# First attention on paired PSUM banks, the convolution's projection four outputs at a time, and the first gathered rows later

## The chip, the cores and the metric

The kernel runs on one core of a Trainium2 chip. Its engines work beside one another, each through its own list of instructions: TensorE (PE) multiplies matrices, VectorE (DVE), ScalarE (ACT) and GpSimd (POOL) do the rest, and the queue of SyncE (SP) issues most transfers. Semaphores alone order them. The metric is the device time of one execution, in microseconds; lower is better.

## The reference

Two transformer blocks on 512 tokens of width 1024, in fp32. The parts that the change touches are in the first:

```
q, k, v, u, ga, gc = split(h @ w_in)               # q: 8 heads, k and v: 2 heads, 256 more keys from the context
p = softmax(q k^T * 128 ** -0.5)                   # 768 keys
y_att = (p v) @ w_attn_o
g = a * sigmoid(b);  g = depthwise_conv(g, 31 taps) + conv_b        # a, b = split(u)
y_conv = silu(layernorm(g)) @ w_conv_o
x = x + g1 * ((sigmoid(ga) * y_att + sigmoid(gc) * y_conv) @ w_out)
x = x + g2 * peer_ffn(modulate(rmsnorm(x)))        # 16384 experts, 128 chosen for each token
```

shift, scale and g1, g2 come from silu(c) @ w_mod, 48 rows of 128. Then a second block of attention (block-sparse and differential) follows, which the change leaves as it is.

## The kernel before

Nearly all products are made as three: each fp32 operand is split into a high half (rounded to fp32r) and a low half (the rest), and TensorE adds high·high, high·low and low·high (mm3, L708). So every weight chunk of 128x1024 goes through a ring: SP loads it into one of 4 raw buffers (L551), ACT makes the high half Rh (ahead, L1236), POOL or DVE makes the low half Rl (lows, L1735; low_half, L1826), and TensorE uses it in 24 matmuls (gemm_T, L720). Rh and Rl have 5 slots. LOW_DVE names the chunks whose low half DVE makes. Rows of w_mod pass through the same raw buffers and are reduced on DVE (modulation, L1875). The order of all chunks is the list of stream_plan; the bank, the count of fills and the count of reads of each PSUM use are worked out ahead in psum_plan.

**First attention.** 32 steps, one for a head and 128 queries. In step n TensorE turns the weights P of step n (turn1), makes the scores of step n+2 (scores1, 512 and 256 columns in two banks), does one whole projection of 24 matmuls if the step has a job (attention_jobs: 12 chunks of w_u for the convolution, 11 of w_g for the gates), and every second step multiplies by the values (values1). DVE finds the maximum of each score row in scores1, hands the negative to ACT (semaphore neg), later the reciprocal of the sum (finish1, pinv). ACT takes the exponential (exps1), divides (normed1), copies the turned weights out (turned1), and empties the job's bank: gate for w_g, glu_gate for the sigmoid half of w_u. Between its steps DVE works through the taps of the depthwise convolution, 31 for each of 8 channel blocks, by tap(), 217 of them in these 32 steps. All jobs use bank 6, so a job starts only when the last one's bank has been emptied.

**Behind it.** w_ao (8 chunks) projects the attention. DVE does the last 31 taps, TensorE sums over channels with a matrix of ones for the mean (mu), DVE subtracts, ACT squares, TensorE sums again (var), DVE and ACT make rsd, and then per channel block DVE multiplies by rsd (cn), ACT does silu and the high half XAh (cRh), DVE and POOL in turn the low half XAl. w_co needs all 8 blocks of XA for each of its 8 outputs. merge_att multiplies the outputs of w_ao by the gates sga. Gates are kept in DRAM meanwhile (store_gate) and come back as sga and sgc, 2 MB each.

**Expert layer.** 128 experts' rows for each of the first 128 tokens are gathered by GpSimd, 4 KB a partition, 0.5 MB a gather, into 7 buffers (gather, L1778): 128 of u, then 128 of v. DVE takes them one by one (gathered, L2380 and L2388). The other 384 tokens go through dense products with all 128+128 chunks, in 16 groups (m) of 12 chunks (n); product and product_low (L2348, L2353) make the moving operand XG, whose high half ACT makes (weighed, L1555). GATHERED says how many rows DVE has taken behind each chunk.

## Time and profile before

| | |
|---|---|
| median of 3 runs | 2286.78 us (2285.72 to 2289.66) |
| the profiled execution | 2285.51 us, span 2283.7 us |
| PE busy | 2139.4 us, 94% |
| PE weight loads busy | 1832.0 us, 80% |
| DVE busy | 1698.7 us, 74% |
| ACT busy | 942.9 us, 41% |
| POOL busy | 964.6 us, 42% |
| granted TensorE clock, mean | 0.978 |
| DMA, mean | 200 GB/s |

"Busy" counts an engine's own instructions; the line numbers are those of the kernel before. A matmul's length in the profile overlaps the next one's, so TensorE's pace is read from the distance between starts. The granted clock is the share of full speed at which TensorE ran.

### The profile page before, as it was taken

Reading aid. Unit: us, or ns where it says so; the run is one execution under the profiler, and the core shown is the slowest. Engines: PE = TensorE matmul, PEld = TensorE weight load, DVE = VectorE, ACT = ScalarE, POOL = GpSimd, SP = SyncE. Lnnn points to the kernel's source line nnn. Section 1 sums busy time; section 2 is a strip of 40 time slices with the busy share of each in tenths; the row PEclk is TensorE's granted clock in tenths of the full one; section 3 lists DMA queues with packets and bytes.
Section 4 is the critical chain, followed back from the end, with each engine's and each line's share of the span. In section 5 each row is a group of like instructions: output and inputs, shape, how many; then the busy total and the mean of one; then the engine's idle time right before and its main releaser. Section 6 shows DMA issues by size and latency. Waiting matters only on the chain. (4 is left out here: it accounts for less than half of the span.)

```text
span 2283.7 us, 29764 instructions
## 1 busy us (share of the span) xinstructions
PE 2139.4 (94%) x10685; PEld 1832.0 (80%) x10685; DVE 1698.7 (74%) x3444; ACT 942.9 (41%) x1544; POOL 964.6 (42%) x633
## 2 busy tenths in 40 slices
PE   6998899896989999989989999999999999899988
PEld 3886677665768999989978988888988888777767
DVE  5876887887460999999868888887888887745243
ACT  3445555434233443444423333333333333445572
POOL 0341122124434565789944444444444542442222
PEclk9999999998999999999999999999999999899999
DMA  7332011154632454546799999999999996221111
GB/s 297 102 93 74 33 61 65 44 187 155 232 131 91 143 162 153 173 153 225 264 359 360 350 336 333 352 353 339 360 359 340 350 359 221 97 80 57 39 56 47
DMA packets 177137, 455.84 MB, mean 200 GB/s; under 512 B 13792, under 2 KB 80736, under 8 KB 175328
## 3 DMA queue, kind: packets, MB, share of 16 engines
q1 hardware_dynamic: 136912, 293.57, 37.7%
q0 software_dynamic: 36864, 134.23, 15.8%
q10 hardware_dynamic: 3216, 26.15, 3.0%
q8 instruction: 86, 1.41, 0.2%
...
## 5 line engine op out<-in xcount | busy, mean ns | idle before, releaser
L1735 POOL TENSOR_TENSOR Rl<-raw,Rh 128x1024 fp32r<-128x1024 f32 x171 | 447.8, 2624 | 795.4 <-ACT Rh L1236 795.0
L709 PE MATMUL bank<-XAh,Rh 128*128 128x384 f32 (+1 forms) x1472 | 537.2, 365 | 38.1 <-POOL Rl L1735 15.3
L1236 ACT ACTIVATE Rh<-raw 128x1024 fp32r<-128x1024 f32 x380 | 399.9, 1056 | 338.5 <-DMA raw<-in_u 108.9
L711 PE MATMUL bank<-XAh,Rl 128*128 128x384 f32 (+1 forms) x1472 | 523.0, 355 | 0.0
L710 PE MATMUL bank<-XAl,Rh 128*128 128x384 f32 (+1 forms) x1472 | 522.8, 355 | 0.0
L709 PEld LDWEIGHTS bank<-XAh,Rh 128*128 128x128 f32 x1472 | 281.3, 191 | 61.6 <-issue 20.0
L710 PEld LDWEIGHTS bank<-XAl,Rh 128*128 128x128 f32 x1472 | 281.3, 191 | 18.2
L711 PEld LDWEIGHTS bank<-XAh,Rl 128*128 128x128 f32 x1472 | 280.3, 190 | 18.4
L1778 POOL DMA_INDIRECT ga<-in_v,eid x128 | 181.3, 1416 | 204.4 <-DVE y L2388 187.0
L1778 POOL DMA_INDIRECT ga<-in_un,eid x128 | 172.7, 1349 | 220.9 <-DVE act L2380 197.1
L1826 DVE TENSOR_TENSOR Rl<-raw,Rh 128x1024 fp32r<-128x1024 f32 x197 | 242.1, 1229 | 2.5 <-ACT Rh L1236 2.5
L1055 PE MATMUL bank<-Rh,XGh 128*128 128x512 f32 x744 | 230.2, 391 | 2.6 <-issue 2.6
L1057 PE MATMUL bank<-Rl,XGh 128*128 128x512 f32 x744 | 229.8, 390 | 0.0
L1059 PE MATMUL bank<-Rh,XGl 128*128 128x512 f32 x744 | 229.7, 390 | 0.0
L2047 DVE SCALAR_TENSOR_TENSOR cout<-gb,vecs,cout 128x512 f32<-128x512 f32 x240 | 206.2, 859 | 2.1
L709 PE MATMUL bank<-Rh,XAh 128*128 128x512 f32 x416 | 166.3, 400 | 3.4 <-DVE Rl L1826 1.8
L2388 DVE SCALAR_TENSOR_TENSOR y<-ga,act,y 128x1024 f32<-128x1024 f32 x127 | 163.1, 1284 | 2.5
L1055 PEld LDWEIGHTS bank<-Rh,XGh 128*128 128x128 f32 x744 | 139.9, 188 | 30.9 <-issue 2.9
L2380 DVE CUSTOM_DVE_ANT_0 ga<-ga,x 128x1024 f32<-128x1024 f32 x128 | 154.3, 1218 | 13.4 <-DMA ga<-in_un,eid 13.4
L1057 PEld LDWEIGHTS bank<-Rl,XGh 128*128 128x128 f32 x744 | 140.0, 188 | 29.4
L1059 PEld LDWEIGHTS bank<-Rh,XGl 128*128 128x128 f32 x744 | 140.0, 188 | 29.3
L711 PE MATMUL bank<-Rh,XAl 128*128 128x512 f32 x416 | 162.8, 391 | 0.0
...
## 6 DMA issues: line engine op xcount, KB each, us to landing
raw<-in_u SPq DMA_DIRECT2D x128, 512.0 KB, 8.3
raw<-in_v SPq DMA_DIRECT2D x128, 512.0 KB, 6.2
...
```

The lines of the kernel that those rows point to most:

```text
L709: e.matmul(o, sh, mh, start=first, stop=False)
L710: e.matmul(o, sh, ml, start=False, stop=False)
L711: return e.matmul(o, sl, mh, start=False, stop=last)
L1055: e.matmul(o[i][:, :], XGh[:, x, tok], hi[:, 512 * i:512 * i + 512], start=first, stop=False)
L1057: e.matmul(o[i][:, :], XGh[:, x, tok], lo[:, 512 * i:512 * i + 512], start=False, stop=False)
L1059: t = e.matmul(o[i][:, :], XGl[:, x, tok], hi[:, 512 * i:512 * i + 512], start=False, stop=False)
L1236: e.activation(Rh[:, r % NRING, :], raw[:, n % NRAW, :], ACT.Copy).then_inc(s["hi"], 1)
L1735: e.tensor_tensor(Rl[:, r % NRING, :], raw[:, n % NRAW, :], Rh[:, r % NRING, :].bitcast(F32), ALU.subtract).then_inc(s["lo"], 1)
L1778: e.indirect_dma_start(ga[n % NGB][:, :], None, table[:, :], bass.IndirectOffsetOnAxis(ap=eid[:, n % 128:n % 128 + 1], axis=0)).then_inc(s ...
L1826: e.tensor_tensor(Rl[:, r % NRING, :], raw[:, c % NRAW, :], Rh[:, r % NRING, :].bitcast(F32), ALU.subtract).then_inc(s["lov"], 1)
L2047: ins = e.scalar_tensor_tensor(out=o, in0=g[:, j:j + 512], scalar=vec("taps", 31 * cb + j), in1=o, op0=ALU.mult, op1=ALU.add)
L2388: t = e.scalar_tensor_tensor(out=y0[:, :], in0=v, scalar=act0[:, j:j + 1], in1=y0[:, :], op0=ALU.mult, op1=ALU.add)
```

## The change

Six edits:

1. The scores of a step lie in one tensor of two banks (pair). DVE takes the negated maximum of all 768 columns in one instruction, ACT one exponential with one sum; the factor 128^-0.5 is multiplied into the gain of q beforehand. The addition of two sums and the maximum of two maxima go.
2. In a step with a job ACT empties the job's bank first and makes the next high half after that. The job of step 0 comes ahead of the first turn on TensorE; the job w_g 15 moves from step 27 to step 31 and has a buffer of its own (pkg3).
3. The low halves of w_ao 3 to 7, w_co 0 to 7 and w_o 0 and 1 move from POOL to DVE, and stand between its taps and layer-norm steps. POOL no longer makes low halves of XA.
4. w_mod rows are read at other places, w_ao 2 and 3 are loaded ahead of sga. TensorE does seven of the w_ao products ahead of mu and none between mu and var.
5. w_co 0 to 3 are worked on together, block by block of XA (24 matmuls become 12 for each of 8 blocks, over four banks), the others one after another.
6. GpSimd gathers rows 5 and later only when the first product is done, and DVE takes one row ahead of it instead of four; the three rows are caught up in groups 4, 6 and 11, in which DVE takes one row more each.

```diff
-    for m, n in zip(range(5, 16), (0, 2, 3, 8, 12, 13, 17, 18, 22, 26, 27)):
+    for m, n in zip(range(5, 16), (0, 2, 3, 8, 12, 13, 17, 18, 22, 26, 31)):
...
-    for i, w in enumerate(("w_ao", "w_co", "w_o", "w_pq")):
-        for m in range(8):
-            p += [(w, m), ("w_mod", 16 + 8 * i + m)]
+    for m in range(8):
+        p += [("w_ao", m), ("w_mod", 16 + m)]
+    p += [("w_co", m) for m in range(4)]
+    for m, mods in zip(range(4, 8), ((24, 25), (26, 27), (28, 29), ())):
+        p += [("w_mod", n) for n in mods] + [("w_co", m)]
+    for m in range(8):
+        p += [("w_o", m)] + [("w_mod", n) for n in ((30 + 2 * m, 31 + 2 * m) if m < 2 else (32 + m,))]
+    for m in range(8):
+        p += [("w_pq", m), ("w_mod", 40 + m)]
...
+        if _m == 0 and _n < 4:
+            _k = (0, 0, 0, 1)[_n]
+        if _m in (4, 6, 9, 10, 11, 12, 13) and _n == 2:
...
+    def scores(n):
+        use(("s", n, 0), 2 * (n % 2), 1, 2)
+        use(("s", n, 1), 2 * (n % 2) + 1, 0, 0)
...
-LOW_DVE = set(range(8)) | set(LATE) | set(range(DENSE, DENSE + 12 * NPARK))
+LOW_DVE = {CH[key] for key in [("w_ao", m) for m in range(3, 8)] + [("w_co", m) for m in range(8)] + [("w_o", 0), ("w_o", 1)]} | set(range(8)) | set(LATE) | set(range(DENSE, DENSE + 12 * NPARK))
...
-        bank = [ctx.enter_context(nc.psum_tensor(f"bank{i}", [128, 512], F32)) for i in range(8)]
+        pair = [ctx.enter_context(nc.psum_tensor(f"pair{i}", [128, 1024], F32)) for i in range(2)]
+        bank = [pair[i // 2][:, i % 2 * 512:i % 2 * 512 + 512] for i in range(4)]
+        bank += [ctx.enter_context(nc.psum_tensor(f"bank{i}", [128, 512], F32)) for i in range(4, 8)]
...
-            loads(CH["w_ao", 1] + 1)
+            loads(CH["w_ao", 3])
             for i in range(3):
                 e.wait_ge(s[f"pkg{i}"], 16 * PKG.count(i))
             e.wait_ge(free[7], USES["y", 31].done)
             e.dma_start(sga[:, :, :], gg[0:8].rearrange("m p t -> p m t")).then_inc(s["sga"], 16)
-            loads(CH["w_ao", 7] + 1)
+            store_gate(15)
+            loads(CH["w_co", 3])
+            e.wait_ge(s["pkg3"], 16)
...
+            gemm_T(jobs[0], XA, ("j", 0))
             for n, job in enumerate(jobs):
                 turn1(n)
                 if n + 2 < 32:
                     scores1(n + 2)
-                if job:
+                if n and job:
...
-            for cb in range(6):
+            for cb in range(7):
...
+            held = [hold(("co", cb)) for cb in range(4)]
+            for k in range(8):
+                conv_ready(k)
+                for cb in range(4):
+                    o, done = held[cb]
+                    hi, lo = chunk(("w_co", cb))
+                    c = slice(k * 128, k * 128 + 128)
+                    t = mm3(o[:, :], hi[:, c], lo[:, c], XAh[:, k, :], XAl[:, k, :], k == 0, k == 7)
+                    if k == 7:
+                        t.then_inc(done, 1)
+            for cb in range(4, 8):
+                gemm_T(("w_co", cb), XA, ("co", cb))
...
-                for j, c0, w in ((0, 0, 512), (1, 512, 256)):
-                    u = USES["s", n, j]
-                    e.activation(P1[i][:, c0:c0 + w], bank[u.bank][:, 0:w], ACT.Exp, bias=ks[:, 3:4], scale=SC1,
-                                 accum_out=ks[:, 4 + j:5 + j]).then_inc(free[u.bank], 1)
+                u = USES["s", n, 0]
+                e.activation(P1[i][:, :], pair[n % 2][:, 0:768], ACT.Exp, bias=ks[:, 3:4], scale=1.0,
+                             accum_out=ks[:, 4:5]).then_inc(free[u.bank], 1)
...
-                if job:
-                    ahead(JOB[n] + 3)
                 if n in GATE_OF:
                     gate(GATE_OF[n])
                 elif job and job[1] >= 8:
                     glu_gate(job[1] - 8)
+                if job:
+                    ahead(JOB[n] + 3)
...
-            ahead(CH["w_ao", 2])
+            ahead(CH["w_ao", 3])
             e.wait_ge(s["sga"], 16)
             for m in range(8):
                 e.activation(sga[:, m, :], sga[:, m, :], ACT.Sigmoid).then_inc(s["sgas"], 1)
-            ahead(CH["w_ao", 7])
+            ahead(CH["w_ao", 6])
             for cb in range(8):
                 e.wait_ge(s["sub"], cb + 1)
                 if cb >= 4:
                     e.wait_ge(s["ltv"], cb - 3)
                 e.activation(lt[cb % 4][:, :], cout[:, cb, :], ACT.Square).then_inc(s["sqc"], 1)
+                if cb == 3:
+                    ahead(CH["w_ao", 7])
             root("conv", rsd[:, :])
+            ahead(CH["w_co", 3])
             for cb in range(8):
                 i = cb % 4
                 e.wait_ge(s["cn"], cb + 1)
                 if cb >= 4:
-                    if cb % 2:
-                        e.wait_ge(s["cRv"], (cb - 4) // 2 + 1)
-                    else:
-                        e.wait_ge(s["cRg"], (cb - 4) // 2 + 1)
+                    e.wait_ge(s["cRv"], cb - 3)
                 e.activation(lt[i][:, :], cout[:, cb, :], ACT.Silu, bias=vec("lnb", cb), scale=vec("lng", cb)
                              ).then_inc(s["sil"], 1)
                 e.wait_ge(s["sil"], cb + 1)
                 e.activation(XAh[:, cb, :], lt[i][:, :], ACT.Copy).then_inc(s["cRh"], 1)
-                if cb == 3:
-                    ahead(CH["w_co", 0])
-            ahead(CH["w_co", 1])
+            ahead(CH["w_co", 4])
...
-            gather(7)
+            e.wait_ge(s["prodl"], 4)
...
+            t_fold = own(e.tensor_scalar(row("qg"), row("qg"), SC1, None, ALU.mult))
+            after(t_fold)
...
-                u0, u1 = USES["s", n, 0], USES["s", n, 1]
-                e.wait_ge(full[u0.bank], u0.full)
-                own(e.tensor_reduce(ks[:, 0:1], bank[u0.bank][:, :], AX, ALU.max))
+                u = USES["s", n, 0]
+                e.wait_ge(full[u.bank], u.full)
+                e.tensor_reduce(ks[:, 3:4], pair[n % 2][:, 0:768], AX, ALU.max, negate=True).then_inc(s["neg"], 1)
                 tap()
-                e.wait_ge(full[u1.bank], u1.full)
-                t = own(e.tensor_reduce(ks[:, 1:2], bank[u1.bank][:, 0:256], AX, ALU.max))
                 tap()
-                after(t)
-                t = own(e.tensor_tensor(ks[:, 2:3], ks[:, 0:1], ks[:, 1:2], ALU.max))
+
+            def finish1(n):
+
+                ks = sml[:, 104 + 8 * (n % 3):112 + 8 * (n % 3)]
+                u = USES["s", n, 0]
+                e.wait_ge(free[u.bank], u.done)
+                e.reciprocal(ks[:, 7:8], ks[:, 4:5]).then_inc(s["pinv"], 1)
...
+            def last_taps(n):
+                while n_taps < 7 * 31 + n:
                     tap()
-                merge_att(i)
+
+            modulation(16, 18)
+            last_taps(10)
+            low_half(CH["w_ao", 3])
+            modulation(18, 20)
+            last_taps(13)
+            low_half(CH["w_ao", 4])
+            last_taps(16)
+            low_half(CH["w_ao", 5])
+            modulation(20, 21)
+            last_taps(24)
+            low_half(CH["w_ao", 6])
+            merge_att(0)
+            modulation(21, 22)
+            last_taps(31)
+            merge_att(1)
...
+            modulation(22, 23)
+            low_half(CH["w_ao", 7])
+            merge_att(2)
+            modulation(23, 24)
             merge_att(3)
-            merge_att(4)
             u = USES["var",]
             e.wait_ge(s["ltv"], 8)
             variance("conv", rsd[:, :], bank[u.bank][:, :], D)
+            merge_att(4)
...
+            conv_normed(0)
+            conv_normed(1)
+            low_half(CH["w_co", 0])
+            low_half(CH["w_co", 1])
+            conv_normed(2)
+            conv_low(0)
+            low_half(CH["w_co", 2])
+            low_half(CH["w_co", 3])
+            for cb in range(3, 8):
+                conv_normed(cb)
+                conv_low(cb - 2)
+            conv_low(6)
+            conv_low(7)
+            merge_att(6)
+            merge_att(7)
             modulation(24, 26)
+            low_half(CH["w_co", 4])
+            modulation(26, 30)
```

Three places of DVE's list, before and after; the line numbers of "now" are those of the changed kernel, and xN stands for N alike in a row.

One step of the attention, before: the two maxima (L2071, L2074), their maximum and its negative, the sum and the reciprocal (L2090), with taps (cout<-gb) between.

```order
L2071 TENSOR_REDUCE sml<-bank 128x1
L2047 SCALAR_TENSOR_TENSOR cout<-gb_112,vecs,cout 128x512
L2074 TENSOR_REDUCE sml<-bank 128x1
L2047 SCALAR_TENSOR_TENSOR cout<-gb_112,vecs,cout 128x512
L2077 TENSOR_TENSOR sml<-sml 128x1
L2047 SCALAR_TENSOR_TENSOR cout<-gb_112,vecs,cout 128x512
L2080 TENSOR_SCALAR sml<-sml 128x1
L2087 TENSOR_TENSOR sml<-sml 128x1
L2047 SCALAR_TENSOR_TENSOR cout<-gb_112,vecs,cout 128x512
L2090 RECIPROCAL sml<-sml 128x1
L2047 SCALAR_TENSOR_TENSOR cout<-gb_112,vecs,cout 128x512
```

The same place now (L2088 is the maximum, L2097 the reciprocal, L2105 the low half of the step's output):

```order
L2097 RECIPROCAL sml<-sml 128x1
L2064 SCALAR_TENSOR_TENSOR cout<-gb_113,vecs,cout 128x512 x2
L2088 TENSOR_REDUCE sml<-pair 128x1
L2064 SCALAR_TENSOR_TENSOR cout<-gb_113,vecs,cout 128x512 x5
L2097 RECIPROCAL sml<-sml 128x1
L2064 SCALAR_TENSOR_TENSOR cout<-gb_113,vecs,cout 128x512 x2
L2088 TENSOR_REDUCE sml<-pair 128x1
L2064 SCALAR_TENSOR_TENSOR cout<-gb_113,vecs,cout 128x512 x5
```

The chain from the scores to the negated maximum went from four instructions with three taps between to one; a step's other taps stand behind it.

The normalisation of the convolution, before: rsd, its product with the blocks of cout (L2152), the low half XAl, rows of w_mod (L1875).

```order
L2148 RECIPROCAL rsd<-rsd 128x512
L2152 TENSOR_TENSOR cout<-cout,rsd 128x512 x2
L2155 TENSOR_TENSOR XAl<-lt_125,XAh 128x512
L1875 ISA raw,mod<-raw,crow 128x1024
L1875 ISA mod 128x1
L1875 ISA raw,mod<-raw,crow 128x1024
L1875 ISA mod 128x1
L2152 TENSOR_TENSOR cout<-cout,rsd 128x512 x2
L2155 TENSOR_TENSOR XAl<-lt_127,XAh 128x512
L2127 TENSOR_TENSOR sga<-sga,bank 128x512
L2152 TENSOR_TENSOR cout<-cout,rsd 128x512 x2
```

Now, with the low halves of w_co (Rl<-raw,Rh) in the same list:

```order
L2174 RECIPROCAL rsd<-rsd 128x512
L2179 TENSOR_TENSOR cout<-cout,rsd 128x512 x2
L1841 TENSOR_TENSOR Rl<-raw,Rh 128x1024 x2
L2179 TENSOR_TENSOR cout<-cout,rsd 128x512
L2183 TENSOR_TENSOR XAl<-lt_125,XAh 128x512
L1841 TENSOR_TENSOR Rl<-raw,Rh 128x1024 x2
L2179 TENSOR_TENSOR cout<-cout,rsd 128x512
L2183 TENSOR_TENSOR XAl<-lt_126,XAh 128x512
L2179 TENSOR_TENSOR cout<-cout,rsd 128x512
L2183 TENSOR_TENSOR XAl<-lt_127,XAh 128x512
L2179 TENSOR_TENSOR cout<-cout,rsd 128x512
```

The four low halves of w_co 0 to 3 stand among the first three products; all low halves of XA are DVE's; the w_mod rows and the merges moved behind them.

The first gathered rows (ga), before, ahead of the first products gt<-gt,wg:

```order
L2380 ISA ga_173,act_179<-ga_173,x_142 128x1024
L2380 ISA act_179 128x1
L1826 TENSOR_TENSOR Rl<-raw,Rh 128x1024
L2380 ISA ga_174,act_179<-ga_174,x_142 128x1024
L2380 ISA act_179 128x1
L1826 TENSOR_TENSOR Rl<-raw,Rh 128x1024
L2380 ISA ga_175,act_179<-ga_175,x_142 128x1024
L2380 ISA act_179 128x1
L2348 TENSOR_TENSOR gt_166<-gt_166,wg_164 128x384 x4
L2353 TENSOR_TENSOR XGl<-gt_166,XGh 128x384 x4
```

Now:

```order
L2425 ISA ga_173,act_180<-ga_173,x_143 128x1024
L2425 ISA act_180 128x1
L1841 TENSOR_TENSOR Rl<-raw,Rh 128x1024 x3
L2393 TENSOR_TENSOR gt_167<-gt_167,wg_165 128x384 x4
L2398 TENSOR_TENSOR XGl<-gt_167,XGh 128x384 x4
L1841 TENSOR_TENSOR Rl<-raw,Rh 128x1024
```

Three of four gathered rows left the place ahead of the first products; row 0 stays.

## Rows read from the trace of the kernel before

**Rows 1.** Windows: stretch, us; busy us of PE, PEld, DVE, ACT, POOL; clock, DMA, GB/s
```profile
181.95:453.63 271.68, 238.80 (x1056) 187.32 (x1057) 224.63 (x429) 143.96 (x291) 55.91 (x22) 0.96 0.16 54
453.63:580.30 126.67, 105.80 (x416) 79.76 (x417) 99.90 (x118) 50.46 (x68) 44.92 (x20) 0.93 0.51 170
...
1580.00:1680.00 100.00, 100.00 (x488) 88.47 (x487) 85.94 (x94) 35.84 (x48) 50.79 (x36) 1.00 0.99 362
```

**Rows 2.** Waits of PE, 181.9 to 454: who for whom, us, times, longest
```profile
PE bank L863 <- ACT P L1402: 14.8, 7, 6.6
PE bank L709 <- ACT gb L1329: 7.6, 3, 4.4
PE bank L709 <- ACT pkg L1338: 4.5, 2, 3.2
PE bank L873 <- DVE XBl L2097: 4.5, 1, 4.5
```

**Rows 3.** Timeline of PE, 454 to 470: start, length, engine, line, operation
```profile
454.43 0.39 PE L709 MATMUL bank<-XBh,Rh 128*128 128x512 f32 x1
...
459.87 0.39 PE L709 MATMUL bank<-XBh,Rh 128*128 128x512 f32 x1
...
468.80 0.63 PE L710 MATMUL bank<-XBl,Rh 128*128 128x512 f32 x1
469.23 0.63 PE L711 MATMUL bank<-XBh,Rl 128*128 128x512 f32 x1
```

**Rows 4.** Groups by line, 190 to 500: busy us, mean ns; the last, whole span
```profile
L2047 DVE SCALAR_TENSOR_TENSOR cout<-gb,vecs,cout 128x512 f32<-128x512 f32 x231 | 199.5, 864 | 2.1
L1402 ACT ACTIVATE P<-P,sml 128x768 f32<-128x768 f32 x31 | 29.2, 943 | 14.7 <-DVE sml L2090 14.7
L2071 DVE TENSOR_REDUCE sml<-bank 128x1 f32<-128x512 f32 x30 | 20.5, 683 | 3.6 <-PE bank L854 3.6
L2074 DVE TENSOR_REDUCE sml<-bank 128x1 f32<-128x256 f32 x30 | 12.4, 415 | 0.0
L1875 DVE CUSTOM_DVE_ANT_0 raw<-raw,crow 128x1024 f32<-128x1024 f32 x6 | 8.7, 1486 | 0.0
...
L1826 DVE TENSOR_TENSOR Rl<-raw,Rh 128x1024 fp32r<-128x1024 f32 x197 | 242.1, 1229 | 2.5 <-ACT Rh L1236 2.5
```

**Rows 5.** Timeline of DVE and ACT in one attention step
```profile
303.98 0.68 DVE L2071 TENSOR_REDUCE sml<-bank 128x1 f32<-128x512 f32 x1
...
308.82 0.69 ACT L1373 ACTIVATE P<-bank,sml 128x512 f32<-128x512 f32 x1 [3.45 <-DVE sml L2080]
```

**Rows 6.** Waits of PE, 454 to 581
```profile
PE bank L709 <- POOL Rl L1735: 18.8, 4, 12.8
```

**Rows 7.** Timeline of DVE and PE up to the layer norm, 447 to 517
```profile
447.77 5.47 DVE L2047 SCALAR_TENSOR_TENSOR cout<-gb,vecs,cout 128x512 f32<-128x512 f32 x7
...
470.67 14.04 DVE L2047 SCALAR_TENSOR_TENSOR cout<-gb,vecs,cout 128x512 f32<-128x512 f32 x10
...
500.07 4.91 DVE L2140 TENSOR_TENSOR cout<-cout,mu 128x512 f32<-128x512 f32 x8
...
504.63 7.03 PE L907 MATMUL bank<-lt,ones 128*128 128x512 f32 x16
...
513.09 3.35 DVE L2148 RECIPROCAL rsd<-rsd 128x512 f32<-128x512 f32 x1
```

**Rows 8.** Waits of all engines, 190 to 500
```profile
ACT Rh L1236 <- DMA raw<-in_w_ao: 29.7, 4, 12.0
```

**Rows 9.** Timeline, first gathered rows, 1155 to 1200
```profile
1155.02 1.23 DVE L2380 CUSTOM_DVE_ANT_0 ga<-ga,x 128x1024 f32<-128x1024 f32 x1 [2.71 <-DMA ga<-in_un,eid]
...
1173.80 1.06 ACT L1236 ACTIVATE Rh<-raw 128x1024 fp32r<-128x1024 f32 x1 [9.07 <-DMA raw<-in_v]
...
1196.12 1.06 ACT L1236 ACTIVATE Rh<-raw 128x1024 fp32r<-128x1024 f32 x1 [8.16 <-DMA raw<-in_u]
...
1199.38 0.69 PE L709 MATMUL bank<-XAh,Rh 128*128 128x384 f32 x1 [3.75 <-DVE Rl L1826]
```

85 lines of the change are left out of this document (30 added, 55 removed).

## The prediction

> **What bounds the kernel.** I read the busy table first: TensorE is busy 94% of the span, so what can be won is its idle time and its time at the lower clock. Then the waits of PE over the span, and where they lie. The reader is to see two dense piles and one small one. In the first attention, 271.7 us long, PE waits 31.4 us in four groups [rows 1, 2]. From the first product of w_ao to the first of w_o, 126.7 us, it waits 18.8 us for low halves that POOL makes, 12.8 of them at once, ahead of w_co [rows 1, 6]. And at the start of the dense expert products it waits 3.75 us for a low half [rows 9]. Later, between 1580 and 1680 us for instance, PE is busy all 100 of 100 us at a granted clock of 1.00 [rows 1]. All this lies on one line, each stage starting from the last, and TensorE is the engine that ends it; so a us taken from an idle stretch is a us at the end.
>
> Pace of PE: 24 matmuls, one chunk, take 459.87 - 454.43 = 5.44 us, 0.227 each. Behind a wait of 3.4 us they start 0.43 apart (469.23 - 468.80) [rows 3]: the clock is at its lower level, 1.2 GHz instead of 2.4, for some 7 to 10 matmuls, which costs about 1.5 us after each wait of 3 us or more. In the attention this happened after three of the waits (I put 3.7 us in all).
>
> **Attention (edits 1 and 2).** What goes per step on DVE: maxima of 0.683 and 0.415 us become one of 768 columns. The two give a slope of 0.268 for 256 columns, so 0.95 [rows 4]; bounds 0.68 (one instruction of 512) and 1.10 (the two together). Three single-column instructions of some 0.15 go as well. For ACT two exponentials with two sums become one; 768 columns in one instruction take 0.94 in L1402 [rows 4]. The busy time saved is not the gain; the delay is. Before, from the first maximum to the exponential went 308.82 - 303.98 = 4.84 us, as taps stood between (one of them 2.3 us long beside POOL), and ACT stood idle 3.45 of it [rows 5]. Now it is one instruction of 0.95: P is ready 3.9 us sooner, and another 1 us sooner as a sum and a tap ahead of the reciprocal go. Of the seven waits for P, 14.8 us, the longest and first is 6.6; the other six make 8.2, 1.4 each [rows 2], so they go, and so do the 7.6 and 4.5 for the emptying of bank 6, since ACT got to it late because of the same wait and because it made a high half first. The first wait, 6.6, is filled by job 0 (5.44) and the shorter chain. The last, 4.5, came from six taps in front of the low half of the output; the moved job gives DVE time for them.
>
> What takes its place? DVE now needs per step 217/32 = 6.8 taps of 0.864 [rows 4], 5.9 us, with 0.95, 0.15 and 0.3 for outputs and gates: 7.3. PE needs (271.7 - 31.4 - 3.7)/32 = 7.4 on average: almost the same. But its steps are uneven: 3.45 without a job, (236.6 - 23 x 5.44)/32, and 8.9 with one, and DVE can be only about one step behind. Steps 4, 7 and 9 are without a job, so over 4 to 9 PE needs 3 x 12.3 = 37, DVE 6 x 7.3 = 44; the one step of lead takes up part of the 7, I take 4 as a stall. Elsewhere pairs with two jobs (17.8 against 14.6) catch up. Three single steps of 0.5, 0.6 at the start, and at the end 2.2, as the last product by the values waits for the copy and low half of the one before it (one bank). Together 8.3 us stay. Gain 31.4 + 3.7 - 8.3 = 26.8. Bounds: 35 if nothing stays, and 18 if stalls of half the old size stay.
>
> The gate ahead of the high half adds a wait in front of ahead(): behind it is queued the high half of the chunk three jobs on, then the copy of the values. The chunk is not wanted for two jobs, 10.9 us, against 1.06 for the high half and at most 3 for POOL's low half. Cost nothing; without that cover up to 4 us for each job (a rival below).
>
> **From w_ao to w_o (edits 3 to 5).** PE's work there is unchanged: 16 chunks x 5.44 = 87.0, and twice 6.9 for the sums [rows 7], 100.8. Before, 126.7: 25.9 idle or slow. Now in order, from the first matmul of w_ao:
> - w_ao 2 and 3 are loaded ahead of sga, which removes the 12.0 us of waiting for the third chunk [rows 8] and PE's first stall of 3.4.
> - DVE up to the mean: 31 taps of 0.78 at full pace [rows 7], 24.3, six w_mod rows, 8.7, four low halves of 1.23 [rows 4], 4.9, two merges, 1.4: 39.3. PE is there after 7 x 5.44 = 38.1 and needs the last block at 44. DVE's taps are 0.78 here and not the 1.40 that ten of them took beside POOL [rows 7].
> - mean ready at 45.0. Its eviction 0.7, the first difference 0.6, the square 0.7 and handing over: PE idle 2.3. The sum of squares to 54.2, w_ao 7 to 59.6.
> - DVE: eight differences to 50.6 [rows 7], two w_mod rows, one low half and two merges to 55.6, the variance 0.7, two merges 1.4, reciprocal 3.35 [rows 7]: 61.0. Two products with rsd, two low halves, a third product, the first XAl: 66.0. PE idle 6.4.
> - From there four banks take 12 matmuls, 2.7 us, for each block, while DVE needs 0.6 + 0.7 for a block: PE is the slower. Some 0.5 us of waiting in the first block, 1.3 us of lower clock. Before, w_co 0 alone had to walk through all blocks at DVE's and ACT's pace.
>
> Idle 2.3 + 6.4 + 0.5 + 1.3 = 10.5, gain 25.9 - 10.5 = 15.4. What this costs: 15 low halves on DVE, 18.4 us. They are hidden as long as DVE has slack of 44 - 39.3 = 5 us ahead of the mean, and behind the last XAl PE has 4 x 2.7 us of blocks left plus w_co 4. Loads decide the bounds: w_co 3 can be loaded only when w_mod 23 has been read, at 55, and ACT makes all four high halves ahead of silu; it must land by 60. If it takes the 12.0 us of the slowest w_ao chunk [rows 8] instead of 5, 7 us go: lower bound 8. Upper bound 18, if the first block is bounded by the reciprocal alone.
>
> The GpSimd page of the Trainium skill (GPSIMD Engine Reference, Specifications) says that GpSimd shares its SBUF interfaces with VectorE, and that instructions of DVE with two SBUF inputs contend. The trace agrees: 14.04 us for ten taps beside low halves on POOL, 5.47 for seven without. Without contention the same move would only add 18.4 us to DVE; with it, ten taps alone pay back 14.04 - 7.8 = 6.2, a third of that.
>
> **First gathered rows (edit 6).** PE's wait of 3.75 at 1199 was for DVE, which had waited for a high half of ACT behind a load: 9.07 us at 1173.8 and 8.16 at 1196.1 [rows 9]. Three gathers of 0.52 MB fewer in flight by 1170 are, at the 362 GB/s of a full stretch [rows 1], 4.3 us; the first load lands that much sooner, and DVE, SP's next loads and the second landing follow. That takes the 3.75, and with it 1.8 us of lower clock; but DVE's early wait for row 2 (2.71) [rows 9] gains nothing, since ACT and the fourth product of u end last there. The gathers held back come at once at 1162 and collide with loads: I take 4.0, bounds -4 (below) and 7.
>
> The DMA page of the skill (DMA: Bandwidth & Descriptors, Issuing engines are not separate DMA queues) says that transfers of all issuers interleave on the same 16 engines. By that rule, postponing bytes removes none, and three gathers come back in groups 4, 6 and 11. The share of DMA between 1580 and 1680 was 0.99, and PE had no idle time. If the engines were full there, 1.57 MB at 362 GB/s would be 4.3 us given back; that is rival 4.
>
> **Sum.** 26.8 + 15.4 + 4.0 = 46.2. 2285.5 (span 2283.7 and 1.8 around it) - 46.2 = 2239.3; the median shown is 1.3 above the profiled execution, so 2240.
>
> **Rivals.**
> 1. The attention is held by DVE. Its 7.3 us per step against PE's 7.4 speak for it, and steps without a job; against it that it had the time before with 0.8 us more each step. Then 17 us of stalls stay instead of 8.3, the gain is 18: 2249. Chance 0.17.
> 2. DVE, which works in order, stands behind late chunks: its low halves in front of the taps take over ACT's 29.7 us of waiting for w_ao [rows 8]. 29.7 less the slack of 5 is 25 us, less what the earlier w_ao 2 and 3 save (12.0 and some 5): 8 us; and w_co 3 another 7. Then 2240 + 15 = 2255. For it: seven loads are now requested by DVE's own progress. Chance 0.10.
> 3. Nearly no stall stays in the attention, and w_co starts 2 us sooner: 2240 - 8.3 - 2 = 2230. Chance 0.12.
> 4. The gathers are given back: 4.0 and 4.3 less: 2248. Chance 0.07.
> 5. Slower: ACT's new order makes the chunk of three jobs on late in each of 23 steps, and PE waits for it. 1.06 and up to 3 us on POOL, 4 us x 23 = 92: 2240 + 92 = 2332, and at half of it still 2286. It decides from the point at which gate, high and low half together last longer than two jobs, 10.9 us; a gate that waits for its package's store could do that, and nothing in the trace shows such a store waited for. Chance 0.02. Less than that, a gain of the kind in 1, 2 and 4 all failing at their bounds (18 + 8 - 4): 2263, still faster.
> 6. The change doesn't do what it says, say the single instruction over two banks is slow: 0.01, about 2286.
>
> The forecast has 0.51. The range reaches from 2228 to 2260: above 2230 and to the second and fourth rival with their bounds. About 0.2% is what a measurement of this kernel can tell from no change, 4.6 us. Faster 0.95, within 0.01 to 0.02, slower 0.035.
>
> **What would show it.** Right: in the attention one maximum of about 0.95 us and under 12 us of waiting of PE; ACT's waits for the negated maximum a third of before; the stage about 245 us. The low halves at full pace on DVE, the taps of the last block near 0.78; PE's wait ahead of w_co near 6 and the way from w_ao to w_o near 111 us. No wait at the second group of u. Wrong: DVE waiting for raw chunks or for ACT's high halves inside its taps, PE waits for Rl in the attention, the first w_co block later than 70 us behind w_ao, or new idle time of PE in groups 4 to 13.

## The result and the profile after

The changed kernel takes 2248.51 us (median of 4, 2246.93 to 2253.25), against 2288.22 for the kernel before on the same chip: ratio 0.9831, 95% interval 0.9812 to 0.9849, so 39.7 us less. The forecast was 2240 and its range 2228 to 2260: the sign and the range hold, 8.5 us of the size do not. The profiled execution of the changed kernel, 2253.25 (span 2251.4), is the slowest of its four, and that of before lies at the fast end of its own, so the two traces side by side show only 32 us. The other 7 are scatter between traces, most of it in code that the change doesn't touch (the table below, and the last section).

TensorE is busy 95% of the span (94% before) and GpSimd 41%. Windows of the trace after; the columns are those of [rows 1], which they answer to.

```profile
182.78:428.19 245.41, 233.17 (x1057) 184.28 (x1056) 221.65 (x303) 137.92 (x228) 56.09 (x23) 0.98 0.18 61
428.19:541.24 113.05, 105.19 (x417) 80.83 (x417) 97.08 (x135) 48.50 (x66) 1.83 (x1) 0.95 0.54 185
1545.00:1645.00 100.00, 100.00 (x487) 88.47 (x486) 85.96 (x93) 36.12 (x49) 53.99 (x36) 1.00 0.99 362
```

The attention is 271.68 - 245.41 = 26.3 us shorter, w_ao to w_o 126.67 - 113.05 = 13.6, and the dense expert products are as full as they were. Waits of PE in the attention of the changed kernel (engine and line, who is waited for, us, times, longest), against [rows 2]:

```profile
PE bank L878 <- ACT P L1423: 9.9, 7, 2.9
PE pair L723 <- DVE XBl L2105: 2.3, 1, 2.3
```

The emptying of bank 6 is waited for no more, and 31.4 us of waiting are 12.2. Groups by line of the changed kernel in this stretch (busy us, mean ns of one, idle time ahead), the maximum and the exponential, which answer to [rows 4] and [rows 5]:

```profile
L2088 DVE TENSOR_REDUCE sml<-pair 128x1 f32<-128x768 f32 x30 | 28.5, 951 | 3.0 <-PE pair L869 3.0
...
L1394 ACT ACTIVATE P<-pair,sml 128x768 f32<-128x768 f32 x32 | 28.9, 903 | 37.1 <-DVE sml L2088 37.0
```

One instruction over two banks takes 0.951 us, and ScalarE stands 37 us for the maximum, and 12.0 more ahead of the table loads of the same line. The same group before had 79.7, and 16.8 ahead of the table loads:

```profile
L1373 ACT ACTIVATE P<-bank,sml 128x512 f32<-128x512 f32 x64 | 36.6, 577 | 79.7 <-DVE sml L2080 79.6
```

From w_ao on, waits of PE in the changed kernel, against [rows 6]: first up to 547.5 (the wait of 2.3 for XBl is the one at the attention's end, already shown), then 541 to 570.

```profile
PE pair L723 <- DVE XAl L2183: 5.6, 1, 5.6
...
PE bank L922 <- ACT lt L1454: 2.3, 1, 2.3
```
```profile
PE pair L723 <- DVE XBl L2219: 3.8, 2, 2.2
PE pair L723 <- POOL Rl L1757: 1.7, 1, 1.7
```

The 12.8 of before are 5.6. New is the line with 3.8: w_o 0 is begun at 541.24 and then waits twice, at 547.08 and 550.23, for low halves of its own input. What stands behind it is read from the timelines of ScalarE, then SyncE, then VectorE and GpSimd:

```profile
542.97 1.06 ACT L1258 ACTIVATE Rh<-raw 128x1024 fp32r<-128x1024 f32 x1 [4.16 <-DMA raw<-in_w_o]
543.93 0.62 ACT L1476 ACTIVATE XBh<-sgc 128x512 fp32r<-128x512 f32 x1
```
```profile
539.31 0.33 SPq L564 DMA_DIRECT2D raw<-in_w_o  x1
550.20 0.38 SPq L632 DMA_DIRECT2D x<-in_x  x1
550.62 0.51 SPq L564 DMA_DIRECT2D raw<-in_w_mod  x1
551.17 0.43 SPq L564 DMA_DIRECT2D raw<-in_w_o  x1
```
```profile
544.58 2.45 DVE L2219 TENSOR_TENSOR XBl<-sgc,XBh 128x512 fp32r<-128x512 f32 x1 [2.15 <-ACT XBh L1476]
```
```profile
544.10 2.38 POOL L1757 TENSOR_TENSOR Rl<-raw,Rh 128x1024 fp32r<-128x1024 f32 x1 [114.08 <-ACT Rh L1258]
```

The load of w_o 2 is issued at 539.31. ScalarE stands 4.16 us for it with the high half of block 6 queued behind (the call of ahead() in the loop of the merged rows), VectorE waits 2.15 for that high half, and then its low half, 0.69 elsewhere, takes 2.45 beside GpSimd's. Block 7 follows as late.

The gathered rows: at the second group of u PE still waits, 3.26 where [rows 9] have 3.75. From the release of the rows held back, 1131, to the landing of that group's first load, 1162, DMA is full (columns as in [rows 1]); 6.82 of the 11.80 MB moved there come through the queue of the gathers.

```profile
1165.11 0.44 PE L723 MATMUL bank<-XAh,Rh 128*128 128x384 f32 x1 [3.26 <-DVE Rl L1841]
```
```profile
1131.00:1162.00 31.00, 30.85 (x137) 25.20 (x135) 22.75 (x37) 6.79 (x10) 16.04 (x13) 1.00 1.01 381
```

### The profile page after: what moved, and what is told of

The parts are those of the page before. It is cut to its first block and busy times, and to the rows that moved or that the text cites. A ratio compares the mean times of both kernels' runs of the same rounds, so it can differ in the third digit from the quotient of the medians.

```text
span 2251.4 us, 29546 instructions
## 1 busy us (share of the span) xinstructions
PE 2136.3 (95%) x10685; PEld 1831.2 (81%) x10685; DVE 1705.4 (76%) x3336; ACT 937.5 (42%) x1480; POOL 929.4 (41%) x614
## 3 DMA queue, kind: packets, MB, share of 16 engines
q0 software_dynamic: 36864, 134.23, 15.9%
## 5 line engine op out<-in xcount | busy, mean ns | idle before, releaser
L723 PE MATMUL bank<-XAh,Rh 128*128 128x384 f32 (+1 forms) x1280 | 458.7, 358 | 9.4 <-ACT gt L1592 4.2
L725 PE MATMUL bank<-XAh,Rl 128*128 128x384 f32 (+1 forms) x1280 | 444.9, 348 | 0.0
L724 PE MATMUL bank<-XAl,Rh 128*128 128x384 f32 (+1 forms) x1280 | 444.7, 347 | 0.0
L725 PEld LDWEIGHTS bank<-XAh,Rl 128*128 128x128 f32 x1280 | 242.2, 189 | 10.5
L1077 PE MATMUL pair<-Rh,XGh 128*128 128x512 f32 x496 | 153.0, 390 | 2.6 <-issue 2.6
L1779 POOL TENSOR_SCALAR ohA<-iota,idx 128x128 f32<-128x128 f32 x192 | 148.7, 793 | 11.4 <-ACT idx L1532 10.0
L1081 PE MATMUL pair<-Rh,XGl 128*128 128x512 f32 x496 | 152.9, 389 | 0.0
L1079 PE MATMUL pair<-Rl,XGh 128*128 128x512 f32 x496 | 152.9, 389 | 0.0
L2393 DVE TENSOR_TENSOR gt<-gt,wg 128x384 f32<-128x384 f32 x128 | 70.8, 555 | 73.9 <-ACT gt L1592 73.9
L2375 DVE TENSOR_SCALAR ohB<-iota,idx 128x128 f32<-128x128 f32 x384 | 117.6, 355 | 0.5 <-PE pair L1059 0.5
L1059 PE MATMUL pair<-ohB,ohA 128*128 128x128 f32 x768 | 107.5, 282 | 7.7 <-DVE ohB L2375 7.7
```

The source lines that it names most:

```text
L723: e.matmul(o, sh, mh, start=first, stop=False)
L724: e.matmul(o, sh, ml, start=False, stop=False)
L725: return e.matmul(o, sl, mh, start=False, stop=last)
L1077: e.matmul(o[i][:, :], XGh[:, x, tok], hi[:, 512 * i:512 * i + 512], start=first, stop=False)
L1079: e.matmul(o[i][:, :], XGh[:, x, tok], lo[:, 512 * i:512 * i + 512], start=False, stop=False)
```

## Experiments

All runs in one table. Three stretches of PE were measured in the trace of each: the attention (start of the first scores to the first product of w_ao), w_ao to the wait for the layer norm's rows, and the expert products (from the end of PE's work ahead of their first product to its end). Ratios are to the kernel before on the same chip.

| kernel | median us | ratio (95%) | attention | w_ao to norm | experts |
|---|---|---|---|---|---|
| before | 2288.2 | 1 | 274.5 | 177.5 | 794.1 |
| e1 attention alone | 2264.0 | 0.989 (0.9864-0.9916) | 249.8 | 178.3 | 795.5 |
| e2 rows as before | 2253.3 | 0.984 (0.9813-0.9866) | 248.4 | 169.3 | 797.8 |
| changed | 2248.5 | 0.9831 (0.9812-0.9849) | 248.2 | 169.6 | 792.0 |
| e0 changed again | 2244.9 | 0.982 (0.9798-0.9841) | 248.2 | 169.3 | 788.5 |
| e3 low halves on GpSimd | 2258.2 | 0.9863 (0.9839-0.9887) | 248.3 | 182.0 | 792.8 |
| e4 w_o 2 after blocks | 2245.7 | 0.9808 (0.9782-0.9833) | 248.0 | 167.8 | 787.8 |
| e8 and w_o 3 ahead of x | 2238.9 | 0.9789 (0.9771-0.9807) | 248.3 | 161.8 | 790.9 |
| e10 and nine rows | 2236.1 | 0.9791 (0.9771-0.9812) | 247.9 | 163.0 | 783.2 |
| e5 maximum in pieces | 2273.1 | 0.9928 (0.9899-0.9957) | 272.7 | 169.1 | 790.1 |
| e6 high half before gate | 2249.1 | 0.9817 (0.9783-0.9851) | 248.2 | 171.0 | 789.7 |
| e7 two jobs as before | 2246.7 | 0.9803 (0.9768-0.9838) | 252.5 | 169.5 | 790.3 |
| e11 VectorE 0.6 more a step | 2267.8 | 0.9918 (0.9884-0.9952) | 266.0 | 169.4 | 790.0 |
| e12 taps ahead of maximum | 2279.1 | 0.9961 (0.9944-0.9978) | 277.2 | 168.1 | 790.0 |

The attention agrees within 0.5 us over the seven runs with the same code there, so an effect of 1 us can be read from it, where the medians' intervals are some 4 to 8 us wide on each side.

**e1: edits 1 and 2 alone** (on the kernel before).

> The kernel before with edits 1 and 2 alone (paired banks, one maximum, one exponential, gate before high half, first job ahead of step 0, last job in step 31); convolution stage and gathers as before. Theory (the stages are in series): the attention takes about 245.5 us against 271.7, and what it gives stays: 2288.2 - 26 = 2262, 0.9885 of before. Then convolution and gathers of the whole change are worth the other 13 us of the 39. Rival (the attention only hands its gain on to the next waits, since the loads of w_ao and the rows of w_mod are the limit there): the attention is as short, but PE's wait for the third chunk of w_ao grows, and the time is 2270 or more.

2264.0, 24.5 less than before. The attention has 24.7 of the 26.3 that it gains in the whole change (where the other 1.6 lie was not followed), and w_ao to the norm is 178.3, near the 177.5 of before: the stages are in series, nothing is handed on. PE waits 3.9 us in w_ao, 3.4 before. The theory holds.

**e2: edit 6 undone.**

```diff
-        if _m == 0 and _n < 4:
-            _k = (0, 0, 0, 1)[_n]
-        if _m in (4, 6, 9, 10, 11, 12, 13) and _n == 2:
+        if _m in (9, 10, 12, 13) and _n == 2:
...
-            e.wait_ge(s["prodl"], 4)
+            gather(7)
```

> The changed kernel with edit 6 undone: gathered rows fetched (7 at once) and used as before. Theory: the edit is worth about 1 us, since the dense expert part's first load of u lands when the queues are empty either way; the wait at the second group of u is 3.3 to 3.8 us in both, and the time is 2249.5 (0.983 of before). Rival of the prediction (edit worth 4.0): 2252.5, 0.9845, with a wait of 3.7 and a lower clock of 1.8 there and none in the changed kernel. Rival 2 (the edit is given back later): 2248 or less, with PE's idle time in groups 4 to 13 of the changed kernel and not here.

2253.3, and 797.8 in the expert stretch. I had taken "1 us" from the pair of traces, and that was wrong. PE waits 5.1 us at the second group of u here, and 1.4 before it (the line "issue", 4.8, is 2.6 in the changed kernel):

```profile
PE bank L721 <- DVE Rl L1839: 5.1, 1, 5.1
PE pair L1075 <- issue: 4.8, 1, 4.8
...
PE pair L1075 <- DVE Rl L1839: 1.4, 1, 1.4
```

With the rows as before the stretch takes 794.1, 795.5 and 797.8 (mean 795.8), with edit 6 in its place ten traces give 787.8 to 792.8 (mean 790.2). So the edit is worth 5.6 us, and no trace of the one kind overlaps one of the other. The changed kernel's own trace, 792.0, happens to be near the slow end and that of before is the fastest of its kind. The medians, 4.7 apart, agree but can't show it alone.

**e3: the 15 low halves back on GpSimd.**

```diff
-LOW_DVE = {CH[key] for key in [("w_ao", m) for m in range(3, 8)] + ...} | set(range(8)) | ...
+LOW_DVE = set(range(8)) | ...
```

> The changed kernel with the 15 low halves of w_ao 3 to 7, w_co and w_o 0 and 1 made by GpSimd again; VectorE's order otherwise the same. Theory 1 (GpSimd's work slows VectorE's beside it): the taps of the last block rise from 0.78 to 1.4 for those that lie beside a low half; five low halves of 2.4 to 2.6 us ahead of the mean cost VectorE 6 us or so, and save it 4 x 1.23 = 4.9 there, so the mean comes 0 to 2 us later, and the rest of the stage, where 8 more lie beside differences and products, is 3 to 6 us longer: 2252 to 2256. Theory 2 (no contention to speak of; VectorE was only short of time): the mean comes up to 4.9 us sooner as far as PE lets it (it has 6 us of slack), and the stage is the same or 2 us shorter: 2246 to 2248.

Theory 1, with its size too small: w_ao to the norm is 182.0, 12.4 longer than in the changed kernel and longer than before, though VectorE is rid of 18 us of work. Over this stretch VectorE is busy 134.6 us, against 126.0 in the changed kernel. That GpSimd takes twice as long for a low half is not what PE waits for: in the stage it waits 0.6 us for one of GpSimd's, and 9.8 and 7.6 for low halves of VectorE (5.6 and 3.8 in the changed kernel). The taps of the last block rise from 0.75 to 1.03 on average, and these two groups more. VectorE from 428 to 560, first e3, then the changed kernel:

```profile
L2215 DVE TENSOR_TENSOR sgc<-sgc,sga 128x512 f32<-128x512 f32 x8 | 14.5, 1811 | 0.8
L2181 DVE TENSOR_TENSOR cout<-cout,rsd 128x512 f32<-128x512 f32 x8 | 11.3, 1438 | 0.0
```
```profile
L2213 DVE TENSOR_TENSOR sgc<-sgc,sga 128x512 f32<-128x512 f32 x8 | 5.5, 693 | 0.8
L2179 DVE TENSOR_TENSOR cout<-cout,rsd 128x512 f32<-128x512 f32 x8 | 5.4, 685 | 0.0
```

The timeline of e3 shows how, VectorE first and then GpSimd:

```profile
511.11 1.28 DVE L2137 TENSOR_TENSOR sga<-sga,pair 128x512 f32<-128x512 f32 x2
...
530.85 2.54 DVE L2215 TENSOR_TENSOR sgc<-sgc,sga 128x512 f32<-128x512 f32 x1
```
```profile
511.50 2.41 POOL L1757 TENSOR_TENSOR Rl<-raw,Rh 128x1024 fp32r<-128x1024 f32 x1 [9.94 <-ACT Rh L1258]
...
530.45 2.39 POOL L1757 TENSOR_TENSOR Rl<-raw,Rh 128x1024 fp32r<-128x1024 f32 x1 [2.24 <-ACT Rh L1258]
```

An addition of two SBUF operands that meets a GpSimd subtraction does not merely run slower: it ends 0.55 us behind GpSimd's end (533.39 against 532.84), as if it had waited for all of it and then taken its own time. Of the two products with one operand in PSUM, the second lies wholly beside GpSimd's work, and both take 0.64.

This is no single case: between w_ao and the norm of e3, 14 such 128x512 instructions of VectorE start within a GpSimd subtraction, and 13 of them end 0.55 us behind its end; of 7 reductions of w_mod rows (128x1024) 6 end 1.08 behind. The two others meet the one subtraction that itself takes 4.07 us instead of 2.4: there GpSimd was held up. The Trainium skill (SBUF — State Buffer, Who interferes with whom) says that a VectorE instruction with two SBUF inputs contends with a GpSimd instruction that reads SBUF, and one with at most one SBUF input, outside VectorE's 2-port modes, doesn't; the trace agrees, 2.54 against 0.69 for the one and 0.64 for the other.

**e4: w_o 2 after the blocks.**

```diff
-                    ahead(min(BY_RING[RING[CH["w_co", cb]] + NRING], CH["w_o", 2]))
+                    ahead(CH["w_o", 2 if cb == 7 else 1])
```

> The changed kernel, but ScalarE makes the high half of w_o 2 behind the last block of the merged rows instead of ahead of block 6. Theory (ScalarE stood 4.16 us on the load of w_o 2 with blocks 6 and 7 queued behind it): both waits of PE inside w_o 0, 1.60 and 2.18, go, and 1.6 us of lower clock with them; 5.4 us less at the end, 2243, unless the wait of w_o 3 (1.73) takes some: 0 to 1.5 back. Rival (VectorE's rows of w_mod at the blocks 4 to 7 are the limit): block 6 and 7 are as late, since VectorE has 2.2 us more per block; PE still waits 2 us or more there, and 2 us or less are won.

Both waits inside w_o 0 are gone, so the theory of their cause holds and the rival (rows of w_mod) falls. But of the 5.4 only 1.8 are left at the norm, since PE now waits at w_o 3:

```profile
PE pair L723 <- DVE XAl L2183: 5.6, 1, 5.6
PE pair L723 <- POOL Rl L1757: 3.1, 1, 3.1
```

3.07 for 1.73, and a lower clock behind it. In its trace SyncE issues the load of w_o 3 at 547.86, right behind that of x (2 MB).

**e8: and the load of w_o 3 ahead of x.**

```diff
-            loads(CH["w_o", 2])
+            loads(CH["w_o", 3])
             e.wait_ge(s["mRl"], 8)
             e.dma_start(x1[:, :, :], ...)
```

> The changed kernel with the high half of w_o 2 behind block 7 (as in e4_w_o_2_after_blocks) and the load of w_o 3 issued ahead of that of x (2 MB). Theory (the wait ahead of w_o 3, 3.07 us in e4, is the load of w_o 3 queued behind x): no wait of 0.5 us or more is left between the first matmul of w_o 0 and the last of w_o 7, and no lower clock there: against the changed kernel 1.60 + 2.18 + 1.73 + 1.6 of clock = 7 us go, and the turning behind it starts 7 us sooner, 2241.5 or 0.980. Rival (x is wanted at once behind w_o, and comes too late now, or the layer norm's wait of 7.50 grows by what is won): 2245, with a longer wait for the residual rows.

161.8 to the norm, 7.8 less than the changed kernel; expected were 7. Waits of PE from 440 to 585:

```profile
PE pair L723 <- DVE XAl L2183: 5.6, 1, 5.6
PE bank L922 <- ACT lt L1454: 2.3, 1, 2.3
```

The norm's wait is 7.50 as always; x comes in time. 0.9789, where the changed kernel beside it has 0.982.

**e10: and nine rows in the first expert group.**

```diff
-        if _m == 0 and _n < 4:
-            _k = (0, 0, 0, 1)[_n]
-        if _m in (4, 6, 9, 10, 11, 12, 13) and _n == 2:
+        if _m == 0 and _n < 8:
+            _k = (0, 0, 0, 1, 1, 1, 1, 1)[_n]
+        if _m in (2, 3, 4, 5, 6, 7, 9, 10, 11, 12, 13) and _n == 2:
```

> e8_w_o_3_ahead_of_x, and 9 gathered rows used in the first expert group and not 13, so 9 + 7 fetched up to its end and not 13 + 7; the four are used in groups 2, 3, 5 and 7. Theory (DMA is full from the release of the gathers to the second group of u, 30 us, and the first load of that group lands at its end): 2.1 MB at 410 GB/s are 5.1 us, so the wait of 3.3 us there goes, with 1 us of lower clock: 3 to 4 us less than e8, 2238, 0.9785. Rival (what is put off comes back: groups 2 to 7 are as full): a wait appears in one of these groups, and the time is that of e8 or 2 us more.

The expert stretch takes 783.2, 7.0 less than the mean of the ten. There is no wait at the second group of u. The high half of its first chunk in e10, and under it that of e2, each in its own trace (ScalarE):

```profile
1142.79 1.06 ACT L1258 ACTIVATE Rh<-raw 128x1024 fp32r<-128x1024 f32 x1 [7.13 <-DMA raw<-in_u]
```
```profile
1164.69 1.06 ACT L1256 ACTIVATE Rh<-raw 128x1024 fp32r<-128x1024 f32 x1 [9.34 <-DMA raw<-in_u]
```

Counted from the stretch's start (1107.66 and 1112.58) that is 35.1 us against 52.1; in the changed kernel it is 1161.86 - 1115.40 = 46.5. (In the changed kernel's own trace that row names PE as the last released, in the other traces with edit 6 the load of u.) Against e8 the load lands 10.3 us sooner: it is issued 4.9 us sooner, 24.6 us behind the stretch's start for 29.5, and takes 10.5 us for 15.9. So fewer gathers leave both a buffer and the DMA engines free earlier, and how much each is worth was not separated. No wait of PE over 0.25 us appears between there and the end of the groups, so the four rows are not given back. By the medians e8 and e10 can't be told apart (2238.9 and 2236.1, nearly equal ratios): one trace speaks for the four rows, no more. Both are faster than the kernel before. Their medians lie 6 and 9 us below that of the changed kernel on the same chip (2244.9), but the intervals of the ratios overlap with its own.

**e5: the maximum in pieces.**

```diff
-                e.tensor_reduce(ks[:, 3:4], pair[n % 2][:, 0:768], AX, ALU.max, negate=True).then_inc(s["neg"], 1)
+                own(e.tensor_reduce(ks[:, 0:1], pair[n % 2][:, 0:512], AX, ALU.max))
+                tap()
+                t = own(e.tensor_reduce(ks[:, 1:2], pair[n % 2][:, 512:768], AX, ALU.max))
...
+                e.tensor_scalar(ks[:, 3:4], ks[:, 2:3], -1.0, None, ALU.mult).then_inc(s["neg"], 1)
```

> The changed kernel, but VectorE makes the negated maximum as before: 512 and 256 columns apart, larger of the two, times minus one, with a tap behind each of the first three; one exponential and the new orders stay. Theory 1 (the length of the chain from scores to P carries the attention's gain): P comes some 3.9 us later, and the six waits of before on it (1.4 to 2 each) come back, the three that are left grow by 1 to 3 each: the attention takes 10 to 18 us longer than 245.4, and the time is 2259 to 2266. Theory 2 (the orders carry it, that is the job ahead of step 0, the job in step 31 and the gate ahead of the high half): 5 us or less, 2250 to 2254.

The attention is 24.5 us longer, nearly all that edits 1 and 2 brought, and more than the 10 to 18 expected. Paired exponential and new orders are worth some 2 us without the short maximum.

**e6: the high half before the gate.**

```diff
+                if job:
+                    ahead(JOB[n] + 3)
                 if n in GATE_OF:
                     gate(GATE_OF[n])
...
-                if job:
-                    ahead(JOB[n] + 3)
```

> The changed kernel, but ScalarE makes the high half of the chunk three jobs on before it empties the job's bank (sigmoid or gate), as before. Theory (the bank is wanted by the next job in a row, and the high half stood in front): PE waits for bank 6 again at the steps with jobs in a row, 1 us at each of some 7 pairs, since P's chain is short now: 2 to 6 us longer, 2251 to 2255. Rival (the order is indifferent once P is early, the waits of 7.6 and 4.5 having come from the late P alone): 0 to 1 us, 2248.5 to 2249.5. Rival 5 of the prediction (gate first makes chunks late): 1 us or more shorter.

248.2 against 248.2: the order is indifferent to the attention's length. The rival holds, and my theory for this experiment falls: the waits of 7.6 and 4.5 for bank 6 [rows 2] had come from the late P. e5 shows the other side of it: with the gate first but P late, PE waits for the same bank again, 6.3 and 2.8. (The 1.4 us that e6 has more behind w_ao were not followed.)

**e7: the two jobs as before** (job 0 behind the turn of step 0, the last w_g in step 27).

> The changed kernel, but job 0 stands behind the turn of step 0 again, and the last w_g job in step 27 and not in 31 (three packages, as before). Theory: the first wait for P comes back at a length of 3.3 to 4 (6.6 less the shorter chain) less the 2.7 that is there now behind job 0, and the last wait, for the low half of the output, grows from 2.3 to 4 or so, with 1.5 us of lower clock behind each: 4 to 7 us longer, 2252 to 2256. Rival (the work is only moved; PE waits as long at another place): within 1 us.

The attention is 4.2 us longer: PE waits 4.44 us for the first P, and 3.61 for the last low half but one. The trace keeps the 4.2 up to the norm; the medians (2246.7, interval of 16 us) don't show them. By the trace the theory holds.

**e11: one more instruction of VectorE per step.**

```diff
+                e.tensor_reduce(ks[:, 1:2], XAh[:, 0, :].bitcast(F32), AX, ALU.max)
```

> The changed kernel with one more instruction of VectorE in each of the 32 steps of the attention: the maximum of 512 columns of a tile in SBUF, some 0.6 us, its result unused. It measures VectorE's slack in the stage. Rival 1 of the prediction (VectorE holds the attention): all of it shows, 32 x 0.6 = 19 us longer. Theory (TensorE holds it, VectorE has less than it can carry in most steps: 7.3 against 7.4 by my sum, so little slack): if the sum is right, (7.9 - 7.4) x 32 = 16 us; if VectorE's time per step is nearer to 6.9, as the gain of 26.3 and the short waits of the changed kernel suggest, 3 us or less.

It takes 0.60 from start to start (262.12 to 262.72), 19.2 in 32 steps, and the attention is 17.7 longer. So nine tenths of what is added to VectorE in every step show at the end. How far that is lack of slack is taken up behind e12.

**e12: three taps ahead of the maximum.**

```diff
+                tap()
+                tap()
+                tap()
                 e.tensor_reduce(ks[:, 3:4], pair[n % 2][:, 0:768], AX, ALU.max, negate=True).then_inc(s["neg"], 1)
-                tap()
-                tap()
```

> The changed kernel with three taps of VectorE ahead of the maximum of each step of the attention and none behind it: the same instructions and the same work of VectorE, but each P comes 2.6 us later. It separates the two things that e5 put back together, 0.45 us of VectorE per step (14 us in all) and a chain longer by some 3 us. From the first scores to the first product of w_ao: 248.25 in the changed kernel, 272.7 in e5. Theory 1 (as I predicted: the delay is the gain, not the busy time): 260 or more. Theory 2 (VectorE's time per step is what counts, since 92% of the added time showed in e11): e5's loss is 13 of VectorE's time and 11 of delay, or the delay costs nothing beside it: between 248 and 252 if VectorE alone binds, 258 to 260 if both add.

The same instructions, and 277.2: 29.0 longer than the changed kernel, longer even than before. Theory 1. Waits of PE in the attention of e12, and ScalarE's idle time ahead of the exponential:

```profile
PE bank L878 <- ACT P L1423: 18.8, 10, 4.9
PE bank L723 <- ACT gb L1351: 8.0, 3, 3.2
PE bank L723 <- ACT pkg L1360: 4.6, 3, 3.0
```
```profile
L1394 ACT ACTIVATE P<-pair,sml 128x768 f32<-128x768 f32 x32 | 28.9, 902 | 105.5 <-DVE sml L2091 105.4
```

These are the waits of before [rows 2], for P and for bank 6. And VectorE, first e12, then the changed kernel, waits for ScalarE in its turn:

```profile
DVE XBl L2106 <- ACT XBh L1416: 29.4, 14, 3.4
DVE sml L2098 <- ACT P L1394: 5.9, 9, 1.1
```
```profile
DVE XBl L2105 <- ACT XBh L1416: 15.4, 9, 4.5
```

The two engines stand in a ring: a late maximum makes ScalarE late, and its late results make VectorE wait 20 us more, which it then lacks.

**VectorE's busy time and the stage's length.** The attention of seven traces (columns as in [rows 1]: the length, then busy us of PE, PEld, DVE, ACT, POOL), in this order: before, changed, e5, e12, e11, e6, e4.

```profile
179.10:453.63 274.53, 241.65 (x1064) 188.76 (x1065) 226.32 (x432) 145.21 (x292) 55.91 (x22) 0.96 0.16 53
179.94:428.19 248.25, 236.01 (x1064) 186.05 (x1065) 222.89 (x304) 139.42 (x229) 56.09 (x23) 0.98 0.18 60
178.98:451.71 272.73, 244.54 (x1064) 190.25 (x1064) 226.67 (x400) 135.59 (x229) 53.35 (x22) 0.95 0.16 55
179.24:456.44 277.20, 243.25 (x1064) 189.22 (x1065) 230.87 (x304) 135.09 (x229) 54.03 (x22) 0.96 0.16 54
177.21:443.16 265.95, 238.60 (x1064) 186.59 (x1065) 248.31 (x336) 139.24 (x229) 57.77 (x23) 0.97 0.17 56
180.08:428.24 248.16, 232.88 (x1064) 184.06 (x1064) 236.10 (x304) 140.09 (x229) 56.47 (x23) 0.99 0.17 60
180.14:428.11 247.97, 232.87 (x1064) 184.24 (x1064) 225.72 (x304) 139.64 (x229) 58.03 (x23) 0.99 0.18 60
```

The change took only 3.4 us from VectorE's busy time (226.3 to 222.9) and 26.3 from the stage. e5 gives back 3.8 of busy time and 24.5 of the stage, e12 8.0 (the same instructions; its taps take longer on average) and 29.0. e11 adds 25.4, its 19.2 and again slower taps, and costs 17.7. And e6 adds 13.2, nearly all of it slower taps (930 ns on average for 867), and costs nothing: VectorE's waits for XBh fall from 15.4 to 3.3 us instead. So what a us more on VectorE costs depends on its place: nothing where VectorE would have waited for ScalarE, and e11's 0.92 is the price of one in every step, behind the maximum and ahead of the next reciprocal. e4 has the changed kernel's code here, and in its trace PE ran at a granted clock of 0.99 and was busy 3.1 us less; its last wait, for VectorE's XBl, grew from 2.3 to 5.2, and the stage is as long. So it is VectorE's last low half that lets PE out of the stage.

## Why the prediction was right, and where it was not

- **The whole.** By stretches the gain is 274.5 - 248.2 = 26.3, 177.5 - 169.6 = 7.9 and 795.8 - 790.2 = 5.6, together 39.8; the medians say 39.7. That they agree so closely is chance, as the medians' interval is 8 us wide. Predicted were 26.8, 15.4 and 4.0, 46.2 in all.
- **Attention, 26.8: right in its size, by the mechanism named.** The delay of P and not the busy time: e12 takes it all back with 8.0 us more of busy time, e5 nearly all with 3.8. Wrong was the picture beside it, that TensorE ends this stage: e4 shows VectorE's last low half ending it, and e11 that time added to VectorE in every step is paid at 0.92 a us. So rival 1 was right that VectorE, in its ring with ScalarE, holds the stage, and wrong that this would leave the gain at 18. Its sum of busy times (7.3 against 7.4) was no measure of slack: e6 carries 13.2 us more at no cost.
- **Emptying of bank 6.** The reason "and because it made a high half first" falls with e6. The late P was the cause (e5, e6), and edit 2's order on ScalarE does nothing for the stage. Its job moves give 4.2 (e7, by one trace).
- **Remaining stalls, 8.3: 12.2.** Two errors met here. PE's idle time in the stage fell from 271.68 - 238.80 = 32.9 to 245.41 - 233.17 = 12.2, by 20.6 and not the 23.1 forecast (31.4 - 8.3). Its busy time for the same matmuls fell by 5.6 at a granted clock of 0.98 for 0.96, where I had 3.7 for the clock. The one error is 2.5 short and the other 1.9 over, so that 26.3 came out so near to 26.8 is partly luck.
- **w_ao to the first product of w_o, 15.4: 13.6.** Mean 46.9 us behind w_ao (45.0), the wait for squares 2.26 (2.3), the wait ahead of w_co 5.6 (6.4), first product of w_o 113.05 behind w_ao (111). Off is the lower clock: 1.7 us behind the wait of 2.3 at w_ao, and 2.2 behind that of 5.6, where I had 1.3.
- **The step that failed is the end of that sum.** It stops at the first product of w_o, as if the stage handed on all it had. From there to the norm the changed kernel takes 56.6 us and the one before 50.8: 5.8 are given back. The prediction weighed w_co 3's load and what the low halves cost VectorE, and did not follow ScalarE's queue into the loop of the merged rows, where the edit had placed the high half of w_o 2 in front of blocks 6 and 7. e4 shows the cause, and e8 that with w_o 3's load ahead of x 161.8 us are possible, 15.7 less than before. That this is near my 15.4 is chance: 13.6 of it lie ahead of w_o, as in the changed kernel, and 2.1 behind (48.7 us to the norm for 50.8), where the kernel before had a wait of its own of 1.9.
- **The 15 low halves.** That VectorE can carry 18.4 us of them held. The contention was underrated: I put 6.2 on ten taps, e3 shows 12.4 at the end of the stage, with differences, products and additions held up as well as taps.
- **First gathered rows, 4.0: 5.6 by thirteen traces.** The sum was near, its reason not: "That takes the 3.75" is wrong. 0.5 to 3.7 us of that wait stay in all ten traces with the edit, since the rows released (at 1131 in the changed kernel) fill DMA up to the landing of u's first load, a collision that I had named and underrated. What is gained lies ahead of it as well, as the 1.4 and 4.8 of waiting in e2's first products. Rival 4 did not show. Put off rows come back in groups 4, 6 and 11, or in seven groups (2 to 7 and 11) in e10; of these eleven traces nine have no wait of PE over 0.25 us from the second group of u to the end of the groups, the other two one each, of 0.67 and 0.82. A DMA share of 0.99 was not a limit there.
- **The signs.** PE's waiting in the attention is 12.2, where I had said under 12; ScalarE's idle time ahead of the exponential, table loads included, is a half of before (49.1 for 96.5) and not a third; at the second group of u there is a wait. The others came out: one maximum of 0.951, the stage 245.4, the last taps at 0.75, 5.6 ahead of w_co, 113 to w_o.
- **The slower rivals.** The gate ahead of the high half made no chunk late (e6, 248.2 both ways). The single instruction over two banks takes 0.951, estimated 0.95.
